# Loop order inside a unit of a split-precision GEMM: K outside, the four column slices inside

## The chip, the cores and the metric

The kernel runs on one core of one Trainium2 chip. The metric is the device time of one execution in microseconds. All times below are of that one core.

## The reference

The reference computes two transformer blocks on 256 tokens of width 2048, in float32. Block one is a convolution branch and a latent attention branch side by side, joined by an output projection, and a gated FFN. Block two is a gated delta rule beside a block attention, a cross attention, and an FFN with a short convolution. Cut to the part that the change touches, it is a chain of products of activations with weight matrices:

```
z  = rmsnorm(x) @ w_in                              # 2048 -> 3392
q  = rmsnorm(q_lat) @ w_uq; kv = rmsnorm(kv_lat) @ w_ukv
x  = x + rmsnorm(concat(conv, attn) @ w_out)
x  = x + rmsnorm((silu(hf @ w_gate) * (hf @ w_up)) @ w_down)          # D_FF 5632
proj = rmsnorm(x) @ w_in_2                          # block two's mixer
x  = x + concat(o_a, o_b) @ w_out_2
x  = x + cross_attention(x, mem)                    # w_xq, w_xkv, w_xo
x  = x + (silu(conv(h @ w_gate_2) + b) * (h @ w_up_2)) @ w_down_2     # D_FF 5632
out = rmsnorm(x)
```

## The kernel before

Everything lies transposed: channels on the partitions, the 256 tokens along the free dimension. Every weight matrix is read once, in tiles `w_raw` of 4 chunks of K (128 rows each) by 512 columns, four tiles deep (SyncE's queue, function `load`).

float32 products are made of three rounded products. ScalarE writes the rounded high part of a weight tile (`w_hi`, line 449, `split_act`), VectorE the remainder (`w_lo`, line 455, `split_dve`), both in halves of a tile, two chunks of K. Such a half is a **unit**: the grain in which TensorE waits for `lo_done` and in which the slots of `w_hi` (four) and `w_lo` (four tiles) come free again. Activations are kept the same way in `x2[:, k, 0, :]` (high) and `x2[:, k, 1, :]` (low), or in `h2` for the FFN's hidden layer.

In the **wide** form of a GEMM, the one that the change touches, a group makes 512 output columns, as four slices of 128, each with its own PSUM bank (`gr["banks"] + m`). The stationary operand is a 128x128 piece of the weights. One matmul of the high weights streams high and low activations at once, 512 columns (line 829), and one of the low weights streams the high activations, 256 columns, into the upper half of the same bank (line 832). I call them H and L below. For a unit of two chunks a slice takes two H and then two L, and the slices follow one another:

```
m0: H(k0) H(k1) L(k0) L(k1)   m1: H H L L   m2: H H L L   m3: H H L L
```

So a unit is 8 H and 8 L, each with a weight load (LDWEIGHTS) of its own. The last matmul of each slice adds one to the semaphore `products`. ScalarE's `split_act` and SyncE's `load` wait on it for all slices of a whole earlier unit (`used`); the evictions wait in `group_ready` for slices of a group's last unit alone (`final`).

The other forms keep another order: **narrow** (lines 838, 840, 841; mix2b, xq, xo, w_out) has three matmuls of 256 columns for each chunk, hi·hi, hi·lo and lo·hi, two slices in one bank; **swap** (lines 815, 817, 818; the value projections) has the activations stationary and streams 512 weight columns three times.

Wide units stand in conv_in, latents, uq, ukv, ffn, down, qkv_a, w_out_2, xkv, ffn_2 and down_2. ffn and ffn_2 run 11 turns of two groups of 8 units, down and down_2 two turns of two groups of 22 units.

In a GEMM that follows a norm, the sums of squares are made by TensorE in the middle of the GEMM (`sums`, lines 1059, 1080, 1093) in bank 3 or 7 (`SUM_BANK`), and VectorE reads them there (line 1136, which adds to `st_var`). If the next group begins right behind them, TensorE waits for `st_var` before it first writes to that bank, which is the bank of its slice m3.

Of the kernel before, what the change touches and what calls it, by code (L numbers as in the profile page):

```python
# [24 lines left out]
P = 128  # L25
T = 256
# [118 lines left out]
def build(nc, A, out):  # L145
    with ExitStack() as ctx:
        def sem(name):
            return ctx.enter_context(nc.semaphore(name))
# [46 lines left out]
        ps = ctx.enter_context(nc.psum_tensor("ps", [P, 8, W], F32))  # L195
# [73 lines left out]
        def slot(g, j):  # L269

            return (j + g.shift) % RAW
# [3 lines left out]
        def x2c(k):  # L275
            return x2[:, k]

        def h2c(k):
# [34 lines left out]
                 x2c, rs_x, form="narrow", column=1),  # L313
            Gemm("w_out_2", 2, [group(w_loop(A["w_out_2"], b * P, 2 * W), 4, out=(xt, 0 + b, 8), kind="add")
                        for b in (0, 4)], x2c),
# [4 lines left out]
                                 banks=4 + 2 * (n % 2)) for n in range(4)], lambda k: x2c(XO2 + k), form="narrow"),  # L320
# [12 lines left out]
        for n, g in enumerate(GEMMS):  # L333
            g.before = GEMMS[n - 1] if n else None
            g.u0, g.p0, g.e0, g.g0, g.f0, g.slot0 = tiles, prods, ops, groups, hidden, list(slots)
            at = 0
# [38 lines left out]
        products = sem("products")  # L375
# [18 lines left out]
        def first_turn(i):  # L394
            return isinstance(i, int) and i == 0
# [40 lines left out]
        def unit(g, u):  # L436

            gr, _ = group_of(g, u // 2)
            return gr, u // 2, slice(HALF * (u % 2), HALF if u % 2 == 0 else gr["kc"]), slice(0, gr["at"][-1] + P)
# [36 lines left out]
        def evicted_by(g, i, gr):  # L476

            return g.e0 + gr["e"] + 2 + i * g.ops
# [257 lines left out]
        FIRST = 3  # L736

        def finish(steps):
            for _ in steps:
                pass  # L740
# [44 lines left out]
        def multiply(pe, g, *stats, between=None, filler=None, at=FIRST + 1):  # L785

            def body(i, first=0, last=g.units):
                for u in range(first, last):
                    if filler and u:
                        next(filler, None)  # L790
                    gr, j, ks, _ = unit(g, u)
                    n, jj = u - 2 * gr["t"], j - gr["t"]
                    final = n == 2 * gr["tiles"] - 1 and gr["kind"] != "part"

                    pe.wait_ge(lo_done, g.u0 + u + 1 + i * g.units)
                    pe.wait_ge(*g.needs(gr["p0"] + jj * gr["kc"] + ks.stop))
                    if g.name == "w_out" and gr["kind"] == "part" and gr["banks"] == 2 and n == 0:

                        pe.wait_ge(tap1, CV * CONV_K + CC - CV)
                    if n == 0:  # L800

                        if not first_turn(i):
                            pe.wait_ge(evicted, evicted_by(g, i, gr) - g.ops)
                        elif gr["free"]:
                            pe.wait_ge(evicted, gr["free"])
                    w_h = lambda k, c: w_hi[:, u % HIS, k - ks.start, c]
                    w_l = lambda k, c: w_lo[:, slot(g, j), k, c]
                    x = lambda k: g.x(gr["p0"] + jj * gr["kc"] + k)
                    first = n == 0 and not (g.name == "w_out" and gr["p0"])
                    if gr["form"] == "swap":  # L810
                        for t in range(TT):
                            bank = ps[:, gr["banks"] + t, :]
                            tok = slice(t * P, (t + 1) * P)
                            for k in range(ks.start, ks.stop):
                                nc.tensor.matmul(bank, x(k)[:, 0, tok], w_h(k, slice(0, W)),  # L815
                                                 start=(n == 0 and k == 0), stop=False)
                                nc.tensor.matmul(bank, x(k)[:, 1, tok], w_h(k, slice(0, W)), start=False, stop=False)  # L817
                                nc.tensor.matmul(bank, x(k)[:, 0, tok], w_l(k, slice(0, W)), start=False,  # L818
                                                 stop=(final and k == ks.stop - 1)).then_inc(products, 1)
                        continue  # L820
                    for m, c0 in enumerate(gr["at"]):
                        cs = slice(c0, c0 + P)
                        if n == 0 and stats and u > FIRST and first_turn(i) and gr["banks"] + m == SUM_BANK[stats[-1]]:

                            pe.wait_ge(st_var, roots_before(stats[-1]) + 1)
                        if gr["form"] == "wide":
                            bank = ps[:, gr["banks"] + m, :]
                            for k in range(ks.start, ks.stop):
                                nc.tensor.matmul(bank, w_h(k, cs), x(k).rearrange("p a n -> p (a n)"),  # L829
                                                 start=(n == 0 and k == 0), stop=False)  # L830
                            for k in range(ks.start, ks.stop):
                                ins = nc.tensor.matmul(bank[:, T:2 * T], w_l(k, cs), x(k)[:, 0, :],  # L832
                                                       start=False, stop=(final and k == ks.stop - 1))
                        else:
                            out_m = ps[:, gr["banks"] + m // 2, m % 2 * T:(m % 2 + 1) * T]
                            last_m = m % 2 == 1 or m == len(gr["at"]) - 1
                            for k in range(ks.start, ks.stop):
                                nc.tensor.matmul(out_m, w_h(k, cs), x(k)[:, 0, :],  # L838
                                                 start=(first and k == 0 and m % 2 == 0), stop=False)
                                nc.tensor.matmul(out_m, w_h(k, cs), x(k)[:, 1, :], start=False, stop=False)  # L840
                                ins = nc.tensor.matmul(out_m, w_l(k, cs), x(k)[:, 0, :], start=False,  # L841
                                                       stop=(final and k == ks.stop - 1 and last_m))
                        ins.then_inc(products, 1)

            def sums():
                if g.e0:

                    pe.wait_ge(evicted, g.e0)
                if stats[0] in MIXED:
                    sum_mixed(pe, stats[0])  # L850
                else:
                    sum_pe(pe, *stats)

            if stats:
                between = (at, sums)
            if between:
                at, extra = between
                body(0, 0, at)
                extra()
                body(0, at)  # L860
            elif g.name == "w_out":
                at = g.units - 2
                body(0, 0, at)
                pe.wait_ge(geared, 12)
                sum_rows(pe, "mix")
                body(0, at)
                sum_quarter(pe, "mix", STATS["mix"][2] - 1)
            else:
                body(0)
            if g.name in STREAM_STAT and g.turns == 2:  # L870

                name, last = STREAM_STAT[g.name], g.groups[-1]
                at = 2 * last["t"] + 6
                body(1, 0, at)
                pe.wait_ge(evicted, evicted_by(g, 1, g.groups[-2]))
                sum_rows(pe, name)
                body(1, at)
                sum_quarter(pe, name, STATS[name][2] - 1)
            elif g.turns > 1:
                with pe.Fori(1, g.turns) as i:  # L880
                    body(i)
            if filler:
                finish(filler)
# [19 lines left out]
        st_var = sem("st_var")  # L903
# [139 lines left out]
        SUM_BANK = {name: 1 if name == "attn" else 6 if name == "mean" else 3 if name in ("q", "kv", "mix", "ff", "mix2", "final") else 7 for name in STATS}  # L1043
# [40 lines left out]
        def sum_mixed(pe, name):  # L1084

            r, before, parts = STATS[name]
            pe.wait_ge(st_done, r)
            pe.wait_ge(squares, squares_before(name) + parts)
            for c in range(4):
                nc.tensor.matmul(sum_out(name), ones[:], sq_buf[(parts - 1) % 2][:, c, :], start=(c == 0), stop=False)  # L1090
            pe.wait_ge(summed, before + parts - 1)
            for k in range(parts - 1):
                ins = nc.tensor.matmul(sum_out(name), ones[:], ssq[:, k, :], start=False, stop=(k == parts - 2))
            ins.then_inc(st_sum, 1)
# [34 lines left out]
        def roots_before(name):  # L1129
            r = STATS[name][0]  # L1130
            return r - (r > STATS["mean"][0])
# [1755 lines left out]
```

## Time and profile before

| | |
|---|---|
| time before, median of 3 runs | 2576.18 us (2573.57, 2576.18, 2576.4) |
| span of the profiled execution, first to last instruction | 2573.2 us |
| the runs' median less that span | 2.98 us |
| TensorE busy | 2498.0 us, 97% of the span, 14958 matmuls |
| VectorE busy | 1647.7 us, 64% |
| ScalarE busy | 1252.4 us, 49% |
| DMA | 436.27 MB, 170 GB/s |
| mean granted TensorE clock | 0.991 of full speed |

The profiled execution is known by its span alone; whatever time it had beyond the span is taken to be the 2.98 us by which the runs' median exceeds it. Busy time of TensorE is no measure of its pace, because a matmul's record is longer than its distance to the next one: the records overlap. The pace is read from the starts of successive matmuls. The timeline prints starts to 10 ns and merges neighbours of one line ("x2").

### The profile page before, as it was taken

To read this page: it belongs to the slowest core of one execution; us is meant where nothing else is said; L and a number is where in the kernel's file an instruction comes from. 1 tells how busy PE (TensorE), PEld (TensorE's weight loads), DVE (VectorE), ACT (ScalarE), POOL (GpSimd) and SP (SyncE) were. 2 spreads that over 40 slices of the span, in tenths; PEclk is the share of its full clock that TensorE was granted. 3 is DMA by queue.
4 is the path that set the end of the run, shared out by engine and by line. 5 is a ranking of instruction groups with operands and counts; after the bars stand their busy time and mean duration, and the time that the engine had idled before them with its cause. 6 is when DMAs were issued, how large, how long until landed. Compare 5 with 4: busy or idle time off the path is not lost.

```text
span 2573.2 us, 37910 instructions
## 1 busy us (share of the span) xinstructions
PE 2498.0 (97%) x14958; PEld 2201.8 (86%) x14958; DVE 1647.7 (64%) x2156; ACT 1252.4 (49%) x1620; POOL 62.8 (2%) x57
## 2 busy tenths in 40 slices
PE   8989898999999999988999999999999999999998
PEld 7878797888888888877889989888888888888886
DVE  6898757656566554547876436866767676665454
ACT  5555555444444443545454345654544444454343
POOL 0000000000000000000003210000000000000000
PEclk9999999999999999999999999999999999999999
DMA  7553254555556555554553345454555555655553
GB/s 244 190 138 115 66 164 132 195 183 192 186 189 190 185 194 166 198 179 136 185 181 105 99 123 180 164 181 147 174 187 193 183 194 182 193 185 191 180 182 130
DMA packets 238146, 436.27 MB, mean 170 GB/s; under 512 B 18568, under 2 KB 34968, under 8 KB 237904
## 3 DMA queue, kind: packets, MB, share of 16 engines
q1 hardware_dynamic: 234496, 423.66, 51.0%
q0 software_dynamic: 2240, 6.80, 0.8%
q10 hardware_dynamic: 1296, 4.19, 0.4%
q8 instruction: 83, 1.36, 0.2%
q14 instruction: 31, 0.25, 0.0%
HBM read 432.51 MB, written 3.69 MB: 170 GB/s over the span
## 4 chain that ended last, share of the span: by engine, by line
PE 89%; DVE 7%; ACT 2%; DMA 1%; issue 1%; SPq 0%; DVEq 0%; ACTq 0%
PE ps L829 46%; PE ps L832 23%; PE ps L838 3%; PE ps L840 3%; PE ps L841 3%; DVE w_lo L455 2%; DVE ar L1276 2%; PE ps L815 1%; PE ps L817 1%; PE ps L818 1%; PE ps L1309 1%; PE ps L2270 1%; PE ps L2276 1%; ACT w_hi L449 1%; DMA w_raw<-in_w_in 1%
## 5 line engine op out<-in xcount | busy, mean ns | idle before, releaser
L455 DVE TENSOR_TENSOR w_lo<-w_raw,w_hi 128x1024 fp32r<-128x1024 f32 (+3 forms) x820 | 994.7, 1218 | 762.5 <-ACT w_hi L449 760.5
L449 ACT ACTIVATE w_hi<-w_raw 128x1024 fp32r<-128x1024 f32 (+3 forms) x820 | 852.2, 1044 | 908.5 <-PE ps L832 786.2
L829 PE MATMUL ps<-x,w_hi 128*128 128x512 f32 x3936 | 1243.6, 397 | 35.3 <-issue 15.0
L832 PEld LDWEIGHTS ps<-x,w_lo 128*128 128x128 f32 x3936 | 742.6, 189 | 176.0
L832 PE MATMUL ps<-x,w_lo 128*128 128x256 f32 x3936 | 775.7, 279 | 0.0
L829 PEld LDWEIGHTS ps<-x,w_hi 128*128 128x128 f32 x3936 | 602.2, 189 | 38.4 <-issue 26.0
L829 PE MATMUL ps<-h,w_hi 128*128 128x512 f32 x1408 | 444.4, 397 | 4.4 <-DVE w_lo L455 4.2
L832 PEld LDWEIGHTS ps<-h,w_lo 128*128 128x128 f32 x1408 | 265.2, 188 | 62.8
L832 PE MATMUL ps<-h,w_lo 128*128 128x256 f32 x1408 | 277.2, 278 | 0.0
L838 PE MATMUL ps<-x,w_hi 128*128 128x256 f32 x768 | 224.3, 292 | 2.2 <-issue 1.3
L829 PEld LDWEIGHTS ps<-h,w_hi 128*128 128x128 f32 x1408 | 215.1, 189 | 5.4 <-DVE w_lo L455 5.2
L841 PE MATMUL ps<-x,w_lo 128*128 128x256 f32 x768 | 218.6, 285 | 0.0
L840 PE MATMUL ps<-x,w_hi 128*128 128x256 f32 x768 | 218.5, 285 | 0.0
L838 PEld LDWEIGHTS ps<-x,w_hi 128*128 128x128 f32 x768 | 148.6, 193 | 5.8 <-issue 2.2
L840 PEld LDWEIGHTS ps<-x,w_hi 128*128 128x128 f32 x768 | 148.7, 194 | 0.3
L841 PEld LDWEIGHTS ps<-x,w_lo 128*128 128x128 f32 x768 | 148.5, 193 | 0.0
L495 ACT ACTIVATE half<-ps 128x512 f32<-128x512 f32 (+1 forms) x152 | 88.5, 592 | 79.8 <-PE ps L832 79.8
L1276 DVE SCALAR_TENSOR_TENSOR ar<-ar,cols 128x255 f32<-128x255 f32 (+29 forms) x180 | 73.9, 473 | 0.6
L955 ACT ACTIVATE x<-xt,cols 128x256 fp32r<-128x256 f32 x80 | 35.6, 497 | 30.2 <-DVE xt L2697 26.7
L970 DVE SCALAR_TENSOR_TENSOR x<-xt,cols,x 128x256 fp32r<-128x256 f32 x80 | 34.8, 481 | 3.8 <-ACT x L955 3.8
L648 DVE TENSOR_TENSOR up<-half,ps 128x512 f32<-128x512 f32 x44 | 30.1, 684 | 11.0 <-ACT half L495 11.0
L648 DVE TENSOR_TENSOR gate<-half,ps 128x512 f32<-128x512 f32 x44 | 29.9, 684 | 10.1 <-ACT half L495 10.1
(336 smaller groups left out, 1671.4 us busy)
## 6 DMA issues: line engine op xcount, KB each, us to landing
w_raw<-in_w_gate SPq DMA_DIRECT2D x88, 1024.0 KB, 5.1
w_raw<-in_w_up SPq DMA_DIRECT2D x88, 1024.0 KB, 5.1
w_raw<-in_w_down SPq DMA_DIRECT2D x88, 1024.0 KB, 5.1
w_raw<-in_w_in SPq DMA_DIRECT2D x79, 1024.0 KB, 5.1
w_raw<-in_w_out SPq DMA_DIRECT2D x32, 1024.0 KB, 5.1
w_raw<-in_w_xkv SPq DMA_DIRECT2D x8, 1024.0 KB, 5.0
w_raw<-in_w_uq SPq DMA_DIRECT2D x18, 256.0 KB, 3.7
w_raw<-in_w_ukv SPq DMA_DIRECT2D x16, 256.0 KB, 3.9
```

The costliest lines, as they stand in the source:

```text
L449: nc.scalar.activation(w_hi[:, u % HIS, 0:ks.stop - ks.start, cs], w_raw[:, slot(g, j), ks, cs], ACT.Copy)\
L455: nc.vector.tensor_tensor(w_lo[:, slot(g, j), ks, cs], w_raw[:, slot(g, j), ks, cs], w_hi[:, u % HIS, 0:ks.stop - ks.start, cs].bitcast(F3 ...
L495: nc.scalar.activation(half[:, c:c + n, h], banks[:, :, h], ACT.Copy).then_inc(half_out, 1)
L648: nc.vector.tensor_tensor(dst(c, n)[:, :, h], half[:, c:c + n, h], banks[:, :, T + h.start:T + h.stop], ALU.add)\
L829: nc.tensor.matmul(bank, w_h(k, cs), x(k).rearrange("p a n -> p (a n)"), start=(n == 0 and k == 0), stop=False)
L832: ins = nc.tensor.matmul(bank[:, T:2 * T], w_l(k, cs), x(k)[:, 0, :], start=False, stop=(final and k == ks.stop - 1))
L838: nc.tensor.matmul(out_m, w_h(k, cs), x(k)[:, 0, :], start=(first and k == 0 and m % 2 == 0), stop=False)
L840: nc.tensor.matmul(out_m, w_h(k, cs), x(k)[:, 1, :], start=False, stop=False)
L841: ins = nc.tensor.matmul(out_m, w_l(k, cs), x(k)[:, 0, :], start=False, stop=(final and k == ks.stop - 1 and last_m))
L955: ins = nc.scalar.activation(x2[:, first + c, 0, :], src(c), ACT.Copy, scale=gain(c))
L970: ins = nc.vector.scalar_tensor_tensor(x2[:, first + c, 1, :], src(c), gain(c), hi, ALU.mult, ALU.subtract)
L1276: nc.vector.scalar_tensor_tensor(y[:, s:T], u[:, 0:T - s], w, y[:, s:T], ALU.mult, ALU.add).then_inc(tap1, 1)
```

## The change

For wide units that are not the last of their group, the two loops change places. The chunks of K are outside and the slices inside, and all H of the unit come before all L:

```
H(k0): m0 m1 m2 m3   H(k1): m0 m1 m2 m3   L(k0): m0 m1 m2 m3   L(k1): m0 m1 m2 m3
```

The instructions, their operands, their number and the increments of `products` (four a unit, on the L of the last chunk) are the same. The wait for `st_var` stands ahead of the slice's first H. The last unit of each group and the narrow and swapped forms stay as they are.

```diff
--- before.py
+++ after.py
@@ -817,6 +817,22 @@
+                        continue
+                    if gr["form"] == "wide" and not final:
+                        banks = range(gr["banks"], gr["banks"] + len(gr["at"]))
+                        for k in range(ks.start, ks.stop):
+                            for bank, c0 in zip(banks, gr["at"]):
+                                if n == 0 and k == 0 and stats and u > FIRST and first_turn(i) and bank == SUM_BANK[stats[-1]]:
+
+                                    pe.wait_ge(st_var, roots_before(stats[-1]) + 1)
+                                nc.tensor.matmul(ps[:, bank, :], w_h(k, slice(c0, c0 + P)), x(k).rearrange("p a n -> p (a n)"),
+                                                 start=(n == 0 and k == 0), stop=False)
+                        for k in range(ks.start, ks.stop):
+                            for bank, c0 in zip(banks, gr["at"]):
+                                ins = nc.tensor.matmul(ps[:, bank, T:2 * T], w_l(k, slice(c0, c0 + P)), x(k)[:, 0, :],
+                                                       start=False, stop=False)
+                                if k == ks.stop - 1:
+                                    ins.then_inc(products, 1)
                         continue
```

## Rows read from the trace of the kernel before

**Rows 1.** The page: busy time of TensorE and the chain that ended last.
```profile
PE 2498.0 (97%) x14958; PEld 2201.8 (86%) x14958; DVE 1647.7 (64%) x2156; ACT 1252.4 (49%) x1620; POOL 62.8 (2%) x57
...
PE 89%; DVE 7%; ACT 2%; DMA 1%; issue 1%; SPq 0%; DVEq 0%; ACTq 0%
```

**Rows 2.** The page's costliest groups: form, count, busy us, mean ns, idle.
```profile
L829 PE MATMUL ps<-x,w_hi 128*128 128x512 f32 x3936 | 1243.6, 397 | 35.3 <-issue 15.0
...
L832 PE MATMUL ps<-x,w_lo 128*128 128x256 f32 x3936 | 775.7, 279 | 0.0
```

**Rows 3.** Windows, second FFN: bounds, length, busy PE, PEld, DVE, ACT, POOL, PEclk.
```profile
1839.00:2290.00 451.00, 451.00 (x2591) 393.51 (x2589) 316.68 (x402) 222.53 (x258) 0.00 (x0) 1.00 0.59 188
```

**Rows 4.** Who TensorE waited for, over the whole span: us, times, longest.
```profile
PE ps L829 <- DVE w_lo L455: 20.8, 12, 3.9
```

**Rows 5.** Timeline of TensorE, ffn_2: start us, length us, engine, line, operation.
```profile
1813.92 0.63 PE L829 MATMUL ps<-x,w_hi 128*128 128x512 f32 x2
1814.39 0.39 PE L832 MATMUL ps<-x,w_lo 128*128 128x256 f32 x2
1814.62 0.63 PE L829 MATMUL ps<-x,w_hi 128*128 128x512 f32 x2
1815.08 0.40 PE L832 MATMUL ps<-x,w_lo 128*128 128x256 f32 x2
...
1899.87 0.62 PE L829 MATMUL ps<-x,w_hi 128*128 128x512 f32 x2
...
2200.13 0.63 PE L829 MATMUL ps<-x,w_hi 128*128 128x512 f32 x2
```

**Rows 6.** Timeline of TensorE, swapped form, a run of 48 matmuls of 512 columns.
```profile
1731.27 0.40 PE L815 MATMUL ps<-w_hi,xm 128*128 128x512 f32 x1
...
1733.11 0.39 PE L818 MATMUL ps<-w_lo,xm 128*128 128x512 f32 x1
...
1741.95 0.39 PE L818 MATMUL ps<-w_lo,xm 128*128 128x512 f32 x1
```

**Rows 7.** Timeline of TensorE, swapped form in ukv, first and ninth matmul.
```profile
213.97 0.40 PE L815 MATMUL ps<-w_hi,x 128*128 128x512 f32 x1
...
215.81 0.39 PE L818 MATMUL ps<-w_lo,x 128*128 128x512 f32 x1
```

**Rows 8.** Timeline of TensorE, narrow form in xq, behind a swapped run.
```profile
1753.58 0.28 PE L838 MATMUL ps<-x,w_hi 128*128 128x256 f32 x1
1753.69 0.28 PE L840 MATMUL ps<-x,w_hi 128*128 128x256 f32 x1
...
1754.53 0.28 PE L841 MATMUL ps<-x,w_lo 128*128 128x256 f32 x1
```

**Rows 9.** Timeline of TensorE, uq: a unit of one chunk, the next one.
```profile
171.76 0.40 PE L829 MATMUL ps<-xq,w_hi 128*128 128x512 f32 x1
...
173.17 0.40 PE L829 MATMUL ps<-xq,w_hi 128*128 128x512 f32 x1
```

**Rows 10.** Timeline of TensorE, rope: f32 matmuls, each recorded twice.
```profile
229.95 1.89 PE L1230 MATMUL ps<-ar,rope_s 128*128 128x256 f32 x8
231.67 1.03 PE L1232 MATMUL ps<-ar,rope_s 128*128 128x256 f32 x4
```

**Rows 11.** Timeline of TensorE at the lower granted clock, start of qkv_a.
```profile
1161.34 0.63 PE L832 MATMUL ps<-x,w_lo 128*128 128x256 f32 x2
...
1162.62 0.63 PE L832 MATMUL ps<-x,w_lo 128*128 128x256 f32 x2
```

**Rows 12.** Timeline of TensorE and VectorE around two sums of squares.
```profile
431.03 0.82 PE L829 MATMUL ps<-x,w_hi 128*128 128x512 f32 x2
...
431.42 0.42 DVE L1136 TENSOR_SCALAR st_v<-ps 128x256 f32<-128x256 f32 x1 [1.53 <-PE ps L1093]
...
181.85 0.73 PE L829 MATMUL ps<-xq,w_hi 128*128 128x512 f32 x2 [0.92 <-DVE ar L1136]
...
186.44 0.50 PE L829 MATMUL ps<-xq,w_hi 128*128 128x512 f32 x1 [2.23 <-DVE w_lo L455]
```

## The prediction

> **What bounds the kernel now.** I read the page first for the engine that matters. TensorE is busy 97% of the span, and it holds 89% of the chain that ended last, against 7% for VectorE [rows 1]. The reader should see that TensorE sets the end, and that its pace, not its waits, is the time. The costliest groups put a size on it: the high matmuls H and the low matmuls L on `x` alone take 1243.6 and 775.7 us of records, and the H stood idle for only 35.3 us [rows 2]. A window of the second FFN shows the same without a gap: 451.00 us long, 451.00 us of TensorE, at the full clock of 2.4 GHz, with VectorE at 316.68 and ScalarE at 222.53 us, so 134 us of slack on VectorE [rows 3]. The waits of H on `w_lo` come to 20.8 us, in 12 places [rows 4].
>
> Since the change only reorders matmuls, the quantity that matters is the distance from one start to the next, and what it depends on. Records are too long for this (397 and 279 ns [rows 2]), so I go to the timeline. In the second FFN two H take 0.47 and 0.46 us, two L take 0.23 [rows 5]: 0.2325 us for an H and 0.115 for an L. Between the slice that starts at 1899.87 and the one at 2200.13 lie 300.26 us; divided by about 0.697 that is 431 slices, so a slice takes 0.6967 us and a unit of four 2.787 us.
>
> At 2.4 GHz the columns alone need 512/2.4 = 213 ns and 256/2.4 = 107 ns, 2.56 us a unit. The other 0.227 us, 14 ns for each matmul, is what a change of order could touch.
>
> **Where else this overhead shows.** A long run of one kind settles. In the swapped form, 512 columns each, the first eight distances take 1.84 us and the following 39 take 8.84 us, 0.2267 each [rows 6]; an earlier GEMM takes 1.84 us for its first eight too [rows 7]. So a run of 512-column matmuls that follows 256-column ones begins dear (1.84 against 8 x 0.2267 = 1.813, 27 ns) and then goes at 0.2267, less than the 0.2325 of H now. A run of 256-column matmuls behaves the other way round: the first distance is 0.11 us, and eight take 0.95 us, so seven at 0.120 each [rows 8], which is more than the 0.115 of L now. H and L in pairs are always in this transition.
>
> **The change, part by part.**
>
> 1. *H in runs of eight.* By rows 6 and 7, 1.84 us for a unit's eight H; now 8 x 0.2325 = 1.86.
> 2. *L in runs of eight.* By rows 8, 0.95 us; now 8 x 0.115 = 0.92, and with the slice's 0.6967 us exact, 2.787 - 1.86 = 0.927.
> 3. *Sum for a unit:* 1.84 + 0.95 = 2.79 us against 2.787. With starts printed to 10 ns, each of the two terms can be 5 to 10 ns off. The first distance of rows 8 can be up to 0.115, so L may be 0.955. I take 2.792, +5 ns a unit. Both gains and losses are real, and nearly cancel.
> 4. *How many units.* Units that change, with four slices and two chunks: conv_in 28, latents 14, uq 6, ukv 2, ffn 154, down 84, qkv_a 42, w_out_2 28, xkv 7, ffn_2 154, down_2 84 = 603; latents has seven more with three slices. Seven units of qkv_a with one slice keep their order. 610 x 5 ns = **+3.1 us**.
> 5. *Units of one chunk* (three in uq) now alternate H and L: four pairs take 1.41 us [rows 9], 0.3525 a pair against 0.3483 where they stand in twos. As runs of four they would save some 10 ns each: nothing.
> 6. *Bank changes.* Each matmul would write another bank than the one before it. In rope the bank changes after every second record: eight records take 1.72 us, 0.215 each, and no second distance is longer than the others as far as the sum tells [rows 10]. In the narrow run the seven distances after the first, over which a bank change falls, stay at 0.120 [rows 8]. I take nothing. Below zero I find nothing that same-bank accumulation costs: the narrow form's 13 ns a matmul above its columns stand as well in the swapped form. Above, 1 ns a matmul, which these rows could hide, is 16 ns a unit and 9.8 us.
> 7. *Semaphores.* The first three increments of `products` in a unit come up to 2 us later, the last one where it was. ScalarE's split and the DMA queue wait for all four of a whole unit, and evictions look at the last unit of a group, which keeps its order. So no one queued behind them is late: nothing. If that cover were gone, each unit could hold back a split by up to 2 us, but VectorE has 134 us of slack in 451 [rows 3].
> 8. *The wait for `st_var`* falls on slice m3, which used to begin after twelve matmuls and now after three. It stands directly behind the sums in conv_in, ffn, qkv_a and ffn_2, and in uq. In ffn the first H starts at 431.03, VectorE has its answer at 431.42 + 0.42 = 431.84 [rows 12], and m3 would now start at about 431.03 + 0.66 + 0.23 = 431.92, its weight load some 0.23 earlier: late by up to 0.15 us. Behind this waiting load stand all other matmuls of the unit, as TensorE's queue is in order. Four such places, at 0.1 us: **+0.4 us** (0 to 0.8). In uq TensorE already waits for `st_var` until 181.85 and now would have nine more matmuls left behind it, some 1.5 us; but it waits again for `w_lo` until 186.44, 2.23 us [rows 12], where VectorE is late from its own work. That stall shrinks by what the first grew: nothing. Without that cover it is +1.5 us.
> 9. *What waits absorb.* Where TensorE runs into a wait for VectorE anyway [rows 4], the units just before it lose nothing: -0.2 us.
>
> Sum: 3.1 + 0.4 - 0.2 = +3.3 us on the profiled execution's 2573.2 + 2.98 = 2576.18 us, which is the runs' median. That gives **2579.5 us**.
>
> **The Trainium skill.** The page "TensorE: Matmul & The Clock Gate", section "Back-to-back issue gap", has a distance of N/2.4 + 2.5 ns for each matmul at full clock, which is 8 x 215.8 + 8 x 109.2 ns = 2.60 us a unit in either order, as an estimate from that page. The rows show 2.787, so the trace doesn't agree with that formula; by it the change would do nothing.
>
> **The rivals.**
>
> - *Each change of size costs, runs are free* (faster). If a unit went at the settled distances throughout, 8 x 0.2267 + 8 x 0.120 = 2.773 us, it would save 13 ns, 8.2 us in all: 2568. For it: pairs H L cost 0.3525 alternating, 0.3483 in twos, 0.3467 settled. Against it: the run's beginning in rows 6 and 7 is dearer than two alternations.
> - *The order doesn't matter*, H and L keep their present distances: 2576. For it: these have held for 431 slices. Against it: the same shapes go at other distances in longer runs [rows 6, 8].
> - *H stays dear and L becomes dear* (slower). H never settles, because its stationary operand is a weight and not an activation as in the swapped form, and L goes at 0.120: 1.86 + 0.95 = 2.81 us, +23 ns, +14 us: 2590. It decides from +8.5 ns a unit, since 610 of those make 5.2 us. Against it: columns, data type and bank use are those of the form that settles.
> - *H settles and L stays cheap* (faster): 1.84 + 0.92 = 2.76, -27 ns, -16 us: 2560. Rows 8 speak against it, being of the very operands that L has.
> - *A price for each bank change*, up to 1 ns a matmul: 2586.
> - *The clock falls.* At the lower of the two levels, 1.2 GHz, a slice takes 1.28 us [rows 11], so a unit 5.12 instead of 2.787; three such units more would make +7 us: 2583. For it: nothing in the rows, TensorE having no gap in the FFN. The page "TensorE: Matmul & The Clock Gate", section "A second HAM failure mode: psum-queue depth-cycling", says that going round the PSUM banks lets TensorE idle in small gaps until its clock drops; by that rule the change is a loss, and no run here shows it so far.
>
> **How the numbers follow.** The forecast, slightly slower at 2577 to 2583, has a chance of 0.50; order without effect 0.16; transitions cost and runs are free 0.14; H dear and L dear 0.07; bank price 0.06; the clock 0.03; H settled and L cheap 0.04. The range goes from 2567 to 2590: it leaves out the 2560 of the one rival and the far half of two others, about 0.1, and some error of each size. A measurement of this kernel tells a change from none at about 0.2%, 5.2 us. Within 0.2% (2571.0 to 2581.3): about 0.37 of the forecast's 0.50, most of order without effect, a third of the free runs, the small bank prices, 0.58 together. Slower: 0.13 of the forecast, and most of the three slower rivals, 0.27. Faster: 0.15.
>
> **What would show it.** In the profile after, in the second FFN: eight H in about 1.84 us with the last three at 0.227 each, then a first L of 0.11 and seven at 0.120; a unit at 2.79. An H that stays at 0.2325 shows the slow rival, an L at 0.115 the fast ones. The record lengths should move too, H down from 397 ns and L up from 279. In uq the wait before m3 should grow and the one until 186.44 shrink. The granted clock should stay at 0.991. The prediction is wrong if bank changes have a price, or if the distances depend on anything other than the columns of the neighbours.

## The result and the profile after

| | before | after |
|---|---|---|
| median of 20 runs | 2576.17 us (2572.76 to 2580.03) | 2579.85 us (2576.9 to 2583.2) |
| ratio, 95% interval | | 1.0017 (1.0011 to 1.0023) |
| span of the profiled execution | 2573.2 us | 2581.4 us |
| its mean granted clock | 0.991 | 0.989 |

The kernel became slower by 0.17%, 4.4 us by the ratio, 3.7 us by the medians. The interval reaches from 0.11% to 0.23%, so the loss is real, though about as small as what a measurement of this kernel can tell from none. The forecast was 2579.5 us.

The page after shows no new bound. TensorE is still busy 97% of the span, with 7 us more, and holds 88% of the chain:

```profile
PE 2504.9 (97%) x14958; PEld 2219.1 (86%) x14958; DVE 1648.3 (64%) x2156; ACT 1254.6 (49%) x1620; POOL 62.8 (2%) x57
...
PE 88%; DVE 8%; ACT 2%; DMA 1%; issue 1%; DVEq 0%; SPq 0%; ACTq 0%
```

The costliest groups answer to [rows 2]. The matmuls of the changed units now have lines 828 (H) and 832 (L); those of each group's last unit, in the old order, have 845 and 848. The columns are form, count, busy us, mean ns and idle:

```profile
L828 PE MATMUL ps<-x,w_hi 128*128 128x512 f32 x3432 | 871.3, 396 | 35.0 <-issue 15.0
...
L832 PE MATMUL ps<-x,w_lo 128*128 128x256 f32 x3432 | 481.5, 283 | 0.0
...
L845 PE MATMUL ps<-x,w_hi 128*128 128x512 f32 x504 | 158.4, 396 | 0.0
...
L848 PE MATMUL ps<-x,w_lo 128*128 128x256 f32 x504 | 99.0, 278 | 0.0
```

Even these long records show what moved. L in a run of eight lasts 283 ns instead of 278: the low matmuls became dearer. H lasts 396 ns in either order, so the drop that the prediction expected in its record doesn't show.

Timeline of TensorE after, in the second FFN, one changed unit and the beginning of a last unit:

```profile
1907.45 2.00 PE L828 MATMUL ps<-x,w_hi 128*128 128x512 f32 x8
1909.29 1.12 PE L832 MATMUL ps<-x,w_lo 128*128 128x256 f32 x8
1910.25 0.63 PE L845 MATMUL ps<-x,w_hi 128*128 128x512 f32 x2
```

From 1907.45 to 1909.29 are 1.84 us for eight H, and from there to 1910.25 are 0.96 us for eight L: 0.95 to 0.96 where starts are printed to 10 ns. The trace keeps starts to the nanosecond. This is the commonest unit of the changed kernel, 189 of 603, beside the commonest of the kernel before, as distances from each start to the next, worked out from those starts:

```
after   H 233 236 228 233 231 226 227 227   L 113 119 120 120 120 120 120 120      sum 2793 ns
before  H 234 235  L 116 113  H 232 231  L 113 120  H 233 236  L 116 112  H 233 230  L 114 119   2787 ns
```

The slices of before are of two kinds that take turns, though each is H H L L: one ends in L of 116 and 113 (or 112) ns, the other in L of 113 and 120 (or 119). This returns below.

Over all units that no wait disturbs, the mean is 2793.3 ns after and 2786.7 ns before. The last units of the groups, whose order didn't change, still take 2786.7 ns in the kernel after. So the loss is in the changed units and nowhere beside them: 603 x 6.6 ns = 4.0 us.

A window of the second FFN has no gap in either kernel, TensorE being busy for all of the 451 us, as in [rows 3]:

```profile
1846.00:2297.00 451.00, 451.00 (x2584) 396.22 (x2583) 316.11 (x399) 222.92 (x258) 0.00 (x0) 1.00 0.58 187
```

**The span's 8.2 us.** The two profiled executions differ by twice what the medians do. Laid side by side matmul by matmul, the excess lies in a few places, chiefly between 1603 and 1640 us of before (+2.7), between 228 and 387 (+1.9), and around 1030 (+1.2), against -1.7 between 1731 and 1814. There TensorE had its lower clock in one of the two and not in the other. Windows after, at two such places, with the granted clock as the third number from the end:

```profile
1634.60:1639.80 5.20, 5.20 (x16) 4.43 (x17) 5.17 (x10) 5.20 (x10) 0.00 (x0) 0.50 0.32 122
1028.00:1034.00 6.00, 5.47 (x21) 4.71 (x22) 2.93 (x4) 2.57 (x5) 0.00 (x0) 0.72 1.01 381
```

The kernel before has 1.00 from 1628 to 1636, and 0.91 from 1780 to 1800, where the kernel after has 1.00. The profiled execution after was also the slowest of the twenty, 2583.2 us. For a change of 4 us one pair of spans is no measure; the distances inside units are.

### The profile page after: what moved, and what is told of

The parts are those of the page before. It is cut to its first block, busy times and chain, and to the rows that moved or that the text cites. A ratio compares the mean times of both kernels' runs of the same rounds, so it can differ in the third digit from the quotient of the medians.

```text
span 2581.4 us, 37910 instructions
## 1 busy us (share of the span) xinstructions
PE 2504.9 (97%) x14958; PEld 2219.1 (86%) x14958; DVE 1648.3 (64%) x2156; ACT 1254.6 (49%) x1620; POOL 62.8 (2%) x57
## 4 chain that ended last, share of the span: by engine, by line
PE 88%; DVE 8%; ACT 2%; DMA 1%; issue 1%; DVEq 0%; SPq 0%; ACTq 0%
PE ps L828 40%; PE ps L832 21%; PE ps L845 5%; PE ps L854 3%; PE ps L856 3%; PE ps L857 3%; PE ps L848 2%; DVE w_lo L455 2%; DVE ar L1292 2%; PE ps L815 1%; PE ps L818 1%; PE ps L817 1%; PE ps L1325 1%; PE ps L2286 1%; PE ps L2292 1%; ACT w_hi L449 1%
## 5 line engine op out<-in xcount | busy, mean ns | idle before, releaser
L828 PE MATMUL ps<-x,w_hi 128*128 128x512 f32 x3432 | 871.3, 396 | 35.0 <-issue 15.0
L828 PEld LDWEIGHTS ps<-x,w_hi 128*128 128x128 f32 x3432 | 622.1, 190 | 149.9 <-issue 25.7
L832 PEld LDWEIGHTS ps<-x,w_lo 128*128 128x128 f32 x3432 | 471.5, 191 | 34.7
L832 PE MATMUL ps<-x,w_lo 128*128 128x256 f32 x3432 | 481.5, 283 | 0.0
L828 PE MATMUL ps<-h,w_hi 128*128 128x512 f32 x1344 | 338.2, 394 | 5.5 <-DVE w_lo L455 5.5
L828 PEld LDWEIGHTS ps<-h,w_hi 128*128 128x128 f32 x1344 | 242.3, 189 | 49.8 <-DVE w_lo L455 6.3
L857 PE MATMUL ps<-x,w_lo 128*128 128x256 f32 x768 | 218.1, 284 | 0.0
L832 PEld LDWEIGHTS ps<-h,w_lo 128*128 128x128 f32 x1344 | 184.2, 191 | 13.2
L832 PE MATMUL ps<-h,w_lo 128*128 128x256 f32 x1344 | 188.1, 283 | 0.0
L845 PE MATMUL ps<-x,w_hi 128*128 128x512 f32 x504 | 158.4, 396 | 0.0
L854 PEld LDWEIGHTS ps<-x,w_hi 128*128 128x128 f32 x768 | 148.3, 193 | 6.4 <-DVE w_lo L455 3.2
L856 PEld LDWEIGHTS ps<-x,w_hi 128*128 128x128 f32 x768 | 148.5, 193 | 0.4
L857 PEld LDWEIGHTS ps<-x,w_lo 128*128 128x128 f32 x768 | 148.3, 193 | 0.0
L848 PEld LDWEIGHTS ps<-x,w_lo 128*128 128x128 f32 x504 | 94.7, 188 | 22.4
L848 PE MATMUL ps<-x,w_lo 128*128 128x256 f32 x504 | 99.0, 278 | 0.0
L845 PEld LDWEIGHTS ps<-x,w_hi 128*128 128x128 f32 x504 | 76.9, 189 | 0.1
```

The costliest lines, as they stand in the source:

```text
L828: nc.tensor.matmul(ps[:, bank, :], w_h(k, slice(c0, c0 + P)), x(k).rearrange("p a n -> p (a n)"), start=(n == 0 and k == 0), stop=False)
L832: ins = nc.tensor.matmul(ps[:, bank, T:2 * T], w_l(k, slice(c0, c0 + P)), x(k)[:, 0, :], start=False, stop=False)
L854: nc.tensor.matmul(out_m, w_h(k, cs), x(k)[:, 0, :], start=(first and k == 0 and m % 2 == 0), stop=False)
```

## The experiments

All are variants of the changed code. Each replaces the two loops by a list `order` of (kind, chunk k, slice m), which is issued as it stands; `products` gets its increment at the last matmul of each slice. Theory A is the one of the prediction: the distance between starts follows from the order of the sizes, 512 and 256 columns, and from nothing else. "Unit" below is the mean over undisturbed units, from the trace's starts in ns.

### Same sizes, other banks: e1_bank_pairs and e2_sizes_in_twos

```diff
# e1: all H, then all L, but both chunks of a slice in a row
+order = [("H", k, m) for m in range(M) for k in K] + [("L", k, m) for m in range(M) for k in K]
# e2: K outside, another bank for each matmul, but H and L in twos
+order = [(kind, k, m) for k in K for a in range(0, M, 2) for kind in "HL" for m in range(a, min(a + 2, M))]
```

> All eight H of a unit first, then all eight L, as in the change, but both chunks of a slice in a row, so that the bank changes after every second matmul and not after each. Theory A (the pace follows from the order of the sizes, 512 and 256 columns, alone): the unit stays at 2.793 us as in the changed kernel, H 233, 236, 228, 233, 231, 227, 227, 227 ns and L 113 and then 120; time 2580 us, 0.15% over before. Theory B (bank changes cost, some 0.4 ns a matmul, which is the whole of the 6.6 ns a unit): about half of the loss goes, unit 2.790, 2578 us. Theory C (the loss comes from streaming the same chunk of activations four times in a row, K outside): the unit falls back to 2.787, 2576 us.

> K outside and the slices inside as in the change, every matmul in another bank than the one before it, but sizes in twos as in the kernel before: H(k0,m0) H(k0,m1) L(k0,m0) L(k0,m1), H(k0,m2) and so on. Theory A (order of sizes alone): 2.787 us a unit as in the kernel before, 2576 us. Theory B (bank changes cost): 2.793 us or more a unit, 2580 us. Theory C (same chunk of activations in a row): 2.79 or more too, 2578 to 2580 us.

Measured: e1 2578.71 us against 2575.98, ratio 1.0011 (1.0002 to 1.0020), unit 2793.3 ns. e2 2575.93 against 2575.98, ratio 1.0000 (0.9991 to 1.0009), unit 2786.7 ns. The times alone can't tell e1 from the middle case of 2578 us. The timelines can. First e1, then e2, both in the second FFN:

```profile
1898.38 2.00 PE L831 MATMUL ps<-x,w_hi 128*128 128x512 f32 x8
1900.22 1.12 PE L834 MATMUL ps<-x,w_lo 128*128 128x256 f32 x8
1901.17 2.00 PE L831 MATMUL ps<-x,w_hi 128*128 128x512 f32 x8
```

```profile
1900.75 0.40 PE L834 MATMUL ps<-x,w_lo 128*128 128x256 f32 x2
1900.98 0.63 PE L831 MATMUL ps<-x,w_hi 128*128 128x512 f32 x2
1901.45 0.39 PE L834 MATMUL ps<-x,w_lo 128*128 128x256 f32 x2
1901.68 0.62 PE L831 MATMUL ps<-x,w_hi 128*128 128x512 f32 x2
```

e1 has 1.84 and 0.95 us, the numbers of the changed kernel, though its bank changes half as often. e2 has 0.23, 0.47, 0.23, those of the kernel before, though its bank changes at each matmul, as in the change, and its chunk only twice a unit (four times in the change, at each matmul in e1 and before). Between 450 and 889 us, e1 loses 0.93 us against before, as the changed kernel does (0.93), and e2 0.00. So neither the banks nor the chunk of activations has any price here. The order of the sizes has all of it.

### Runs of four: e4_fours

```diff
+order = [(kind, k, m) for k in K for kind in "HL" for m in range(M)]
```

> Runs of four: H(k0) of the four slices, L(k0) of the four, then the same for k1. Theory A with the beginning of a run as the price: H 233, 236, 228, 233 = 930 ns and L 113, 119, 120, 120 = 472 ns, two of each are 2.804 us a unit, 17 ns over before, 610 units: +10.5 us, 2587 us, slower than both runs of two and runs of eight. Rival D (each change of size has a price of its own and the rest of a run is at the settled distances): between the two kernels or below, as four changes a unit stand between eight and two; 2576 to 2580 us.

Measured: 2585.33 us against 2575.98, ratio 1.0043 (1.0029 to 1.0057); unit 2806.4 ns. The timeline of one unit:

```profile
1906.54 1.09 PE L831 MATMUL ps<-x,w_hi 128*128 128x512 f32 x4
1907.47 0.63 PE L834 MATMUL ps<-x,w_lo 128*128 128x256 f32 x4
1907.94 1.09 PE L831 MATMUL ps<-x,w_hi 128*128 128x512 f32 x4
1908.87 0.64 PE L834 MATMUL ps<-x,w_lo 128*128 128x256 f32 x4
1909.35 0.63 PE L847 MATMUL ps<-x,w_hi 128*128 128x512 f32 x2
```

Four H take 0.93 us both times, and four L 0.47 and 0.48. Runs of four are slower than runs of two and than runs of eight. This refutes rival D, a price for each change of size: it has no way to be dearest in the middle. 603 x 19.7 ns are 11.9 us, against 11.1 us by the ratio. The unit is 2.4 ns dearer than theory A's 2804, because its two halves are not alike: in the commonest unit the second four L take 117, 120, 120, 120 ns, the first four 117, 119, 118, 117, though both stand behind four H. What a run costs depends on more than the run ahead of it.

### Runs of sixteen: e5_serpentine

```diff
+order = [(kind, k, m) for kind in ("HL" if n % 2 == 0 else "LH") for k in K for m in range(M)]
```

> The change, but in every second unit the L come first and then the H, so that runs are sixteen long and begin half as often. Theory A: for two units H 1.840 + 8 x 0.2267 and L 0.953 + 8 x 0.120 us = 5.567 us, so 2.783 a unit, 10 ns below the changed kernel and 3 below the one before: 2574 us, 0.08% under before. Rival (the loss has nothing to do with where runs begin): 2.793 a unit, 2580 us. If the first L at a unit's start meets its wait for the low weights later than H would, a little time comes back nowhere, since both wait at the unit's start.

Measured: 2574.74 us against 2575.98, ratio 0.9998 (0.9989 to 1.0007), which doesn't tell it from the kernel before. The trace does. Timeline, from an H-first unit after a group's last one:

```profile
1905.84 2.00 PE L831 MATMUL ps<-x,w_hi 128*128 128x512 f32 x8
1907.68 2.08 PE L834 MATMUL ps<-x,w_lo 128*128 128x256 f32 x16
1909.60 2.68 PE L831 MATMUL ps<-x,w_hi 128*128 128x512 f32 x11
```

Sixteen L take 1.92 us, so 0.120 each with 7 ns off at the first. Units that continue a run of H take 2766 ns, units that begin one 2801, together 5567: 2783.5 a unit, as forecast. The distances in a continued run are 227, 226, 227 from its first H on.

### Eight patterns in one run: e6_patterns

```diff
+PATS = {("ffn", 0): "HHHLLLHHHLLLHHLL", ("ffn", 1): "HHHHHHLLLLLLHHLL", ("down", 0): "HHLHHLHHLHHLLLLL",
+        ("down", 1): "HHLLLHHLLLHHLHHL", ("ffn_2", 0): "HL" * 8, ("ffn_2", 1): "HLHHLLLHHLHHLLLH",
+        ("down_2", 0): "HHLLLLHHHHHHLLLL", ("down_2", 1): "HHHHHLLLLLHHHLLL"}   # others, and n == 0: HHLL x4
```

> A look, no time to compare: each group of ffn, down, ffn_2 and down_2 has another order of its eight H and eight L (runs of three, of six and two, HHL four times and then five L, HL in turn, and mixtures). Theory A, with the price counted from the beginning of each H run (+6, +9, +1, +6, +4 ns over 227, then nothing) and -7 to -12 ns at the first L of a run: runs of three 2.80 us a unit, runs of six and two about 2.79, HHL four times between 2.79 and 2.81, HL in turn 2.82. No order of whole units goes under the 2.773 us that settled distances give. If one of them goes well under 2.787, it is the version to build.

Measured (mean of undisturbed units with two of their kind ahead of them; the run's time is no comparison):

```
HHLLLLHHHHHHLLLL  2773.3 ns     HHLHHLHHLHHLLLLL  2806.7
HL x 8            2773.3 (*)    HHLLLHHLLLHHLHHL  2826.5
HHHHHHLLLLLLHHLL  2780.0        HLHHLLLHHLHHLLLH  2826.7
HHHHHLLLLLHHHLLL  2793.3
HHHLLLHHHLLLHHLL  2796.6
(*) in ten of the eleven groups; the other one took 2819 to 2830 a unit
```

Between the cheapest and the dearest lie 53 ns, though each has eight H and eight L. The lowest value is that of settled distances throughout, 8 x 226.7 + 8 x 120 = 2773.3, and nothing goes below it. HL in turn was a miss: 2.82 was expected, from [rows 9]. And a price for the beginning of each H run, which theory A had added to the order of the sizes, fails in both directions. By it both 2826 patterns would be far lower, between 2785 and 2805, and HH LLLL HHHHHH LLLL would be near 2795 where it takes 2773.3. In that pattern the six H behind four L take 235 and then 227 at once.

### H and L in turn: e3_alternate

```diff
+order = [(kind, k, m) for k in K for m in range(M) for kind in "HL"]
```

> H and L in turn, eight times a unit, each pair in its own bank. Theory A (the order of sizes alone, the beginning of a run being what is dear): as in the one-chunk units of the kernel before, where four pairs took 1.41 us, so 2.82 us a unit, 34 ns over before, +20.6 us on 603 units and a little on the rest: 2597 us. Rival D (the price falls with shorter runs, as runs of eight and four are dearer than two): below 2.787 us a unit, under 2576 us.

Measured: 2574.26 us against 2574.67, ratio 0.9996 (0.9987 to 1.0005). The expectation of 2597 failed, and the trace shows why. The alternation has two steady cycles. Timelines of one unit in each, first and next start:

```profile
454.33 0.40 PE L831 MATMUL ps<-x,w_hi 128*128 128x512 f32 x1
...
457.16 0.40 PE L831 MATMUL ps<-x,w_hi 128*128 128x512 f32 x1
...
1004.10 0.40 PE L831 MATMUL ps<-h,w_hi 128*128 128x512 f32 x1
...
1006.88 0.40 PE L831 MATMUL ps<-h,w_hi 128*128 128x512 f32 x1
```

```
long cycle   H 232 L 118  H 241 L 120  H 236 L 113, repeated       353.3 ns a pair, 2819 to 2831 a unit
short cycle  H 233 L 117  H 231 L 113, repeated                    346.7 ns a pair, 2773 to 2774 a unit
```

Of the 603 units about 480 stand in the short cycle and nearly 90 in the long one; most others are disturbed by a wait or by the lower clock; a cycle persists until another pattern or a wait interrupts it. 480 x -13.4 and 88 x +40.4 ns make -2.9 us, within the interval. [Rows 9] had caught the long cycle, four pairs of it, and the prediction took this for what alternation costs.

### The alternation entered otherwise: e9_alternate_twos_first

```diff
+if n == 0:      # e3, with the first unit of a group in the old order
+    order = [(kind, k, m) for m in range(M) for kind in "HL" for k in K]
```

> H and L in turn as in the third experiment, but HH LL in the first unit of each group. In the third experiment the alternation stood in one of two cycles, 2.773 us a unit in 482 units and 2.82 to 2.83 in 88, and kept it until a unit in twos came. Theory E (the cycle is chosen by the state at entry, and the unit in twos ahead leads to the short one, as it did in all of the second FFN's first groups in the run with eight patterns): nearly all 527 units at 2.773 us, 7.0 us less than before, 2569 us. Rival (the choice is by chance or by something else): again a tenth or more of the units at 2.82 to 2.83 us, 2572 to 2576 us.

Measured: 2593.77 us against 2575.03, ratio 1.0076 (1.0062 to 1.0090). The opposite of what I expected of theory E. Nearly all units are in the long cycle, here 2.82 us from a unit's start to the next:

```profile
1004.50 0.40 PE L833 MATMUL ps<-h,w_hi 128*128 128x512 f32 x1
...
1007.32 0.40 PE L833 MATMUL ps<-h,w_hi 128*128 128x512 f32 x1
```

Some 37 units are in the short cycle, over 470 in the long. Their sum over the kernel before is 18.4 us; the ratio says 19.6. So the two cycles are real, and which one is entered is systematic, not chance, since one order of the first units gives nearly all of one kind. In e6 the same first unit led to the short cycle in ten groups of eleven (not in all, as the expectation has it), with another pattern's group ahead of it.

The traces show what goes with the choice. Slices H H L L come in the two kinds named above, and they take turns. At each place in e3, e6 and e9 where the alternation follows such a slice undisturbed by waits and by the lower clock, 127 in all, its kind tells the cycle, as distances in ns:

```
slice ahead ends in L 116 (115) 112 (113)    short cycle, 67 of 67 places (e3 54, e6 10, e9 3)
slice ahead ends in L 113 (114) 120 (119)    long cycle,  60 of 60 places (e3 4, e6 1, e9 55)
```

A unit has four slices, so a unit in twos ends in the kind that the slice ahead of it had, and hands that on. In e9 this is nearly always the second kind, in ffn_2 of e6 the first. So the nearest neighbours' sizes don't fix a distance: the pace carries a state over many matmuls. No run changes this state alone, and theory E's reason, that a unit in twos as such leads to the short cycle, was wrong.

### The settled pattern as a kernel: e7_settled

```diff
+pat = "HHHHHHLLLLLLHHLL" if n == 0 else "HHLLLLHHHHHHLLLL"
+order = [(kind, *next(hs if kind == "H" else ls)) for kind in pat]     # hs, ls: (k, m), K outside
```

> An order chosen from the run with eight patterns: HH LLLL HHHHHH LLLL in every unit that is not the first or last of its group, which took 2.7733 us a unit there, and HHHHHH LLLLLL HH LL (2.780 us) in the first unit of each group. Theory A (the order of the sizes alone sets the pace): 527 units save 13.4 ns and 76 save 6.7 ns against the kernel before, 7.6 us in all, and some 0.4 us go to the waits at the sums: 2568 to 2569 us, 0.28% under before. Rival (the low values of the look were a matter of its own neighbours and do not carry over): 2780 ns a unit or more, 2572 us or more.

Measured: 2573.22 us against 2575.03, ratio 0.9989 (0.9980 to 0.9998): faster than the kernel before by 0.5 to 5 us (and so than the changed one, by the units of both), but less than the 7.6 expected. The undisturbed units, carried over to all 603, give 5.0 us. One unit in the first FFN:

```profile
636.36 0.63 PE L836 MATMUL ps<-x,w_hi 128*128 128x512 f32 x2
636.83 0.63 PE L839 MATMUL ps<-x,w_lo 128*128 128x256 f32 x4
637.29 1.53 PE L836 MATMUL ps<-x,w_hi 128*128 128x512 f32 x6
638.66 0.64 PE L839 MATMUL ps<-x,w_lo 128*128 128x256 f32 x4
639.13 0.40 PE L836 MATMUL ps<-x,w_hi 128*128 128x512 f32 x1
```

It goes from 636.36 to 639.13, 2.77 us. The steady units are at 2773 to 2774 ns, so the rival, 2780 or more, is wrong, though the time of 2573.22 us lies in its range and not in theory A's. What the expectation missed are the two ends. Behind a last unit in the old order the group's first unit takes 2798 ns, not 2780, and behind that the next takes 2796, not 2773. A group of eight units, between starts 128 matmuls apart, takes 22.293 us before, 22.340 after and 22.247 in e7: 46 ns saved where 87 (6 x 13.4 + 6.7) were forecast.

### The wait at the sums: e8_first_unit_back

```diff
+if n == 0:      # the change, but the first unit of each group in the old order
+    order = [(kind, k, m) for m in range(M) for kind in "HL" for k in K]
```

> The change, undone in the first unit of each group, so that the wait for the sums of squares stands behind twelve matmuls again. A look at four places. If that wait is the cause of the long distance of 307 ns in those units, it goes away: the first unit behind the sums of ffn takes 2.989 us as in the kernel before instead of 3.069, at four places 0.3 us in all, and the 1.2 us stall in uq is back at its old size. The other units stay at 2.793 us. In the time too little to see.

Measured: a single run, 2579.39 us. The wait for `st_var` stands directly behind the sums at four places besides uq. The first unit there, after and in e8 (each with the start of the next matmul behind it):

```profile
433.85 2.29 PE L828 MATMUL ps<-x,w_hi 128*128 128x512 f32 x8
435.97 1.11 PE L832 MATMUL ps<-x,w_lo 128*128 128x256 f32 x8
436.92 0.40 PE L828 MATMUL ps<-x,w_hi 128*128 128x512 f32 x1
```

```profile
433.36 0.82 PE L833 MATMUL ps<-x,w_hi 128*128 128x512 f32 x2
434.02 0.40 PE L836 MATMUL ps<-x,w_lo 128*128 128x256 f32 x2
...
436.35 0.63 PE L833 MATMUL ps<-x,w_hi 128*128 128x512 f32 x2
```

After, the unit takes 436.92 - 433.85 = 3.07 us; in ns the four take 3071, 3076, 3069 and 3069, with one H in the middle at 307 or 314. In e8 they take 2978 once and 2989 three times, as before, and the long H is gone. That is 0.31 us in all, beyond the 6.6 ns that each loses anyhow. The other units stay at 2793.3 ns. In uq the waits in e8 are 0.82 us for `st_var` and 2.23 for `w_lo`, the size that they had before (0.92 and 2.23).

## Why the prediction was right, point by point

1. **The pace sets the time.** Shown. The waits of the wide form did not grow, except the one in uq (point 8): those on `w_lo` come to 20.8 us in 12 places, as in [rows 4]. In the narrow form one wait on `w_lo` went from 0.9 to 1.9 us, and idle time without a releaser from 1.3 to 0.4. TensorE's waits after:

```profile
PE ps L828 <- DVE w_lo L455: 20.8, 12, 3.6
...
PE ps L828 <- DVE ar L1152: 2.2, 1, 2.2
```

2. **Eight H in 1.84 us, eight L in 0.95.** Right, to the nanosecond of the swapped and narrow runs that they were read from, though those have other operands. e1 and e2 show why that reading carries over: operands and banks don't count here, the order of the columns does. But the prediction's last sentence goes further: it calls itself wrong if the distances depend on anything other than the columns of the neighbours. In that general form it failed. Among H and L in turn all neighbours are the same, and a pair takes 346.7 or 353.3 ns (e3, e9); even H H L L has two kinds. In runs of eight nothing of it shows, where nearly all undisturbed units take 2793 or 2794 ns.
3. **The sum, +5 ns a unit.** Measured +6.6. The value taken was low by 1.6 ns, 1 us in all. The rounding had left the sign open: 1.84 + 0.95 is 3 ns above 2.787, and each term could be 5 to 10 ns off. That the slower side came out was in part luck as the sum was made. It need not have been: the trace of before has the starts of the same two samples in ns, 233 + 236 + 228 + 233 + 230 + 227 + 227 + 226 = 1840 and 113 + 7 x 120 = 953, together 2793.
4. **603 units and seven of three slices.** 603 were found in the trace.
5. **Units of one chunk: nothing.** They are too few to show. But the 0.3525 us a pair that stood there, and served as evidence for the rival "each change of size costs", was the long cycle of an alternation that also goes at 0.3467 (e3). The rival was wrong, as was this reason for it; e4 refutes it.
6. **Bank changes: nothing.** Shown by e1 and e2. The upper bound, 9.8 us, was needlessly wide.
7. **Semaphores: nothing.** Argued from the code; in accord with it the window of the second FFN has no gap after either.
8. **The wait for `st_var`: +0.4 us.** 0.31 measured (e8 and the units above). In uq the first half came as forecast, 1.33 us more against "some 1.5". Timeline after:

```profile
179.42 1.05 PE L828 MATMUL ps<-xq,w_hi 128*128 128x512 f32 x3
182.72 2.29 PE L828 MATMUL ps<-xq,w_hi 128*128 128x512 f32 x5 [2.25 <-DVE ar L1152]
184.81 1.83 PE L832 MATMUL ps<-xq,w_lo 128*128 128x256 f32 x8
186.47 1.09 PE L828 MATMUL ps<-xq,w_hi 128*128 128x512 f32 x4
```

The wait before m3 grew from 0.92 us to 2.25, and the next one, 2.23 us until 186.44 in [rows 12], is gone: no idle time stands at 186.47. But the first wait alone would have left 0.9 us of it. The rest went to the clock, which was granted at 0.50 from 183.0 to 186.4 us, so that eight L took 1.66 us there. e1, whose wait stands behind six matmuls, has the clock at 1.00 from 178 to 190 us, and shows the trade without it:

```profile
182.07 0.73 PE L831 MATMUL ps<-xq,w_hi 128*128 128x512 f32 x2 [1.51 <-DVE ar L1154]
...
186.65 2.11 PE L831 MATMUL ps<-xq,w_hi 128*128 128x512 f32 x8 [1.49 <-DVE w_lo L455]
```

There the first wait grew by 0.59 us and the second shrank by 0.74 (with one of 0.21 us behind it). So the cover is shown. Over the stretch from 167 to 228 us of before, the kernel after loses 0.02 us in all, with the lower clock twice in either.

9. **What waits absorb: -0.2 us.** Below what a run can show here.

The sum was +3.3 us; the units give +4.0, the sums' waits +0.3, and the medians +3.7. The forecast of 2579.5 us lies 0.35 from the measured 2579.85, closer than its terms were known. The Trainium skill's formula in "TensorE: Matmul & The Clock Gate", section "Back-to-back issue gap", which it gives for an isolated matmul, makes 2.60 us for a unit as an estimate and agrees with none of these orders, of which the fastest takes 2.773. The Trainium skill's warning on the same page, in "A second HAM failure mode: psum-queue depth-cycling", didn't come true in the FFNs, where the granted clock stayed 1.00 with each matmul in another bank; the lower mean of 0.989 is also that of the profiled executions of e1 and e2, and e2 lost no time.

## What to carry to other kernels

Where one engine is busy all the time with matmuls that each load their own weights, read the distances between starts, not the records' lengths, and look for the same shapes in another order elsewhere in the trace: they priced this reordering to 1 us before it was made. Where the sum is a small difference of large terms, take the starts in ns, since those printed to 10 ns leave even its sign open. Take such a sample from many repetitions, since four pairs in one place can sit in a cycle that isn't the usual one. And don't expect a gain from spreading neighbouring matmuls over PSUM banks or from reusing the streamed operand: here both were worth nothing, and grouping equal sizes in eights cost 0.17%.

## What the runs showed of the hardware

- At 2.4 GHz each matmul with its weight load takes 13.3 ns more than its columns when settled (226.7 against 213.3, 120.0 against 106.7; wide, narrow and swapped form). At 1.2 GHz it takes its columns alone: 427 and 213.5 ns, a slice in 1.28 us [rows 11].
- Mixed sizes don't settle at once. Behind eight L, H needs five matmuls (233, 236, 228, 233, 231) before 227, and the first L behind eight H comes early (113). In HH LLLL HHHHHH LLLL one H of 235 is enough. The dependence on run length isn't monotonic: a unit takes 2773 or 2820 to 2831 ns with runs of one, 2786.7 with two, 2796.6 with three (and one pair), 2806.4 with four, 2793.3 with eight, 2783.5 with sixteen.
- One and the same sequence, H and L in turn, has two steady cycles, 346.7 and 353.3 ns a pair. Which one is entered goes with the kind of the last H H L L slice ahead, in 127 of 127 places.
- All these unit times lie whole steps of about 6.67 ns above the settled 2773.3: none, 1 (2780.0), 2 (2786.7), 3 (2793.3), 5 (2806.4) and 8 (2826.7); threes and sixteens lie 3.5 and 1.5 above, whole steps over two units, and three pairs of the long cycle lie 3 above the settled 1040 ns.
- The mechanism behind these distances stays open: the runs give its numbers and exclude banks and the streamed chunk, but don't show it.
